# Two transformer blocks on one core: the streamed buffers at other offsets from the weights

## What is computed

```python
# first block
u = rmsnorm(h, norm_mix_pre_w)
q, k, v, z, xbc, dt_raw, gate_logits = split(u @ w_in)
att = dilated_attention(q, k, v) @ w_att_proj      # 12 heads, three dilations
ssm = mamba2_mixer(z, xbc, dt_raw) @ w_ssm_proj    # 32 heads, 8 groups
h = h + rmsnorm((g_att * att + g_ssm * ssm) @ w_out)
f = square(relu(rmsnorm(h) @ w_up)) @ w_down       # 4096 hidden
h = h + rmsnorm(f)
# second block
u_a, u_b, hq, hk, hv, hg = split(rmsnorm(x) @ w_in_2)
y = concat(conformer_conv(u_a, u_b), retention(hq, hk, hv, hg)) @ w_out_2
x = x + rmsnorm(y)
f = (silu(h @ w_ffn_gate_2) * (h @ w_ffn_up_2)) @ w_ffn_down_2   # 2816 hidden
x = x + rmsnorm(f)
x = x + rmsnorm(sigmoid(x @ w_ple_gate_2) * (p @ w_ple_proj_2))
```

## Time and profile before

| | before |
|---|---|
| median of 3 runs | 1813.76 us (1812.43 to 1813.91) |
| the profiled execution's own time | 1813.86 us |
| its span, first to last instruction | 1811.8 us |
| mean granted TensorE clock | 0.998 |
| TensorE busy | 1779.5 us |
| VectorE, ScalarE, GpSimd busy | 841.8, 758.4, 766.4 us |

### The profile page before, as it was taken

How to read it: one execution, slowest core, us unless ns; L and a number is a source line. 1 busy time by engine, 2 the same in 40 slices (tenths; PEclk the granted TensorE clock), 3 DMA queues, 4 the chain that set the end, 5 groups by cost and what they waited for, 6 DMA issues and landing times.

```text
span 1811.8 us, 25066 instructions
## 1 busy us (share of the span) xinstructions
PE 1779.5 (98%) x9062; PEld 1467.6 (81%) x9062; DVE 841.8 (46%) x1577; ACT 758.4 (42%) x1248; POOL 766.4 (42%) x590
## 2 busy tenths in 40 slices
PE   7999999999999999999999999999999999999998
PEld 5777788888888888888888888887778888888877
DVE  4555545677766311273111123899947433320044
ACT  5544554566664322353323233534455332222253
POOL 4322344333333554445444444353233444445543
PEclk9999999999999999999999999999999999999999
DMA  5212233332323222233232322232122232233321
GB/s 186 70 60 83 81 105 111 106 108 95 101 98 128 93 93 97 90 112 111 93 103 93 100 97 82 70 105 70 59 70 73 91 100 97 93 104 105 105 82 47
DMA packets 47803, 170.68 MB, mean 94 GB/s; under 512 B 5312, under 2 KB 7488, under 8 KB 47456
## 3 DMA queue, kind: packets, MB, share of 16 engines
q1 hardware_dynamic: 44352, 156.25, 25.9%
q10 hardware_dynamic: 3360, 13.17, 2.1%
HBM read 167.24 MB, written 2.16 MB: 93 GB/s over the span
## 4 chain that ended last, share of the span: by engine, by line
PE 94%; DVE 4%; ACT 1%; issue 0%; DMA 0%; DVEq 0%; SPq 0%; POOLq 0%; POOL 0%; ACTq 0%
PE bank L395 28%; PE bank L397 28%; PE bank L396 28%; PE bank L574 1%; PE bank L722 1%; PE bank L583 1%; PE bank L596 1%; DVE xs L1879 1%; PE bank L507 1%; PE bank L726 1%; PE bank L706 1%; DVE u_lo L1884 1%; PE bank L822 0%; PE bank L840 0%; PE bank L433 0%
## 5 line engine op out<-in xcount | busy, mean ns | idle before, releaser
L368 POOL TENSOR_TENSOR w_lo<-raw,w_hi 128x512 fp32r<-128x512 f32 x578 | 759.5, 1336 | 1019.2 <-ACT w_hi L1001 1019.0
L395 PE MATMUL bank<-u_hi,w_hi 128*128 128x512 f32 (+1 forms) x1624 | 624.9, 385 | 7.4 <-DVE u_lo L1884 6.5
L397 PE MATMUL bank<-u_hi,w_lo 128*128 128x512 f32 (+1 forms) x1624 | 612.4, 377 | 0.0
L396 PE MATMUL bank<-u_lo,w_hi 128*128 128x512 f32 (+1 forms) x1624 | 611.6, 377 | 0.0
L1001 ACT ACTIVATE w_hi<-raw 128x1024 fp32r<-128x1024 f32 x289 | 303.8, 1052 | 282.5 <-PE bank L397 282.2
L395 PEld LDWEIGHTS bank<-u_hi,w_hi 128*128 128x128 f32 x1624 | 305.5, 188 | 67.9 <-DVE u_lo L1884 7.7
L397 PEld LDWEIGHTS bank<-u_hi,w_lo 128*128 128x128 f32 x1624 | 305.4, 188 | 57.3
L396 PEld LDWEIGHTS bank<-u_lo,w_hi 128*128 128x128 f32 x1624 | 305.8, 188 | 53.5 <-issue 0.5
L395 PE MATMUL bank<-v_hi,w_hi 128*128 128x512 f32 (+1 forms) x368 | 134.4, 365 | 0.2 <-DVE v_lo L2445 0.2
L396 PE MATMUL bank<-v_lo,w_hi 128*128 128x512 f32 (+1 forms) x368 | 133.4, 362 | 0.0
L397 PE MATMUL bank<-v_hi,w_lo 128*128 128x512 f32 (+1 forms) x368 | 133.3, 362 | 0.0
(11 more groups left out here) (320 smaller groups left out, 2175.3 us busy)
## 6 DMA issues: line engine op xcount, KB each, us to landing
raw<-weights SPq DMA_DIRECT2D x289, 512.0 KB, 3.3
bc<-acs ACTq DMA_DIRECT2D x16, 512.0 KB, 4.0
xs<-x SPq DMA_DIRECT2D x4, 512.0 KB, 5.4
xs<-x ACTq DMA_DIRECT2D x1, 2048.0 KB, 7.8
rt<-ret_tables ACTq DMA_DIRECT2D x1, 1536.0 KB, 6.4
out<-xs SPq DMA_DIRECT2D x12, 128.0 KB, 1.8
dist<-att_tables SPq DMA_DIRECT2D x1, 512.0 KB, 10.7
p_raw<-p ACTq DMA_DIRECT2D x1, 512.0 KB, 7.2
```

Of the source, the lines that this page charges most:

```text
L368: return nc.gpsimd.tensor_tensor(w_lo[:, slot, w], raw[:, slot, w], w_hi[:, slot, w].bitcast(F32), ALU.subtract)
L395: mm(dst, w_hi[:, slot, w], hi, start=first, stop=False)
L396: mm(dst, w_hi[:, slot, w], lo, start=False, stop=False)
L397: return mm(dst, w_lo[:, slot, w], hi, start=False, stop=last)
```

## The change

Three areas of `work` are shifted by less than 512 bytes, and with them the tiles in them. No other line changes; the instructions, their order, their semaphores and the DMAs are the same.

- m_at, g_at (and tail, which is g_at + 32 KB) get 256 bytes more: att_acc, mix_hi, logits, p_t, post, hd, acs_h, zz, y_hi, xd, xw, k_t, q_t, b_tok, v_tok, states, v_t, gm and the first half of mix_lo.
- v_at and t_at get 128 bytes more: v_hi, v_lo, wide, glu, tmp, p_raw, the rot and r_ tiles placed from t_at, x_scale, ple_tanh.
- h_hi gets 64 bytes more, h_lo and h_tmp 192.
- raw, w_hi, w_lo, u_hi, u_lo, xs, s_hi, s_lo, the constants, y, y_lo, att_hi, att_lo, dist, bias, cat31, cv, rt, ffn_acc and pj stay.

```diff
-    m_at = work + 32 * K
+    m_at = work + 32 * K + 256
     att_acc = place("att_acc", [P, C8, T], at=m_at)
     mix_hi = place("mix_hi", [P, C8, T], F32R, at=m_at)
...
-    g_at = work + 48 * K
+    g_at = m_at + 16 * K
     post = place("post", [P, 8, T], at=g_at)
...
-    v_at = work + 40 * K
+    v_at = work + 40 * K + 128
     v_hi = place("v_hi", [P, C8, T], F32R, at=v_at)
     v_lo = place("v_lo", [P, C8, T], F32R, at=v_at + 16 * K)
-    t_at = work + 72 * K
+    t_at = v_at + 32 * K
...
-    h_hi = place("h_hi", [P, H2, T], F32R, at=work)
-    h_lo = place("h_lo", [P, H2, T], F32R, at=work + 44 * K)
-    h_tmp = place("h_tmp", [P, T], at=work + 88 * K)
+    h_hi = place("h_hi", [P, H2, T], F32R, at=work + 64)
+    h_lo = place("h_lo", [P, H2, T], F32R, at=work + 44 * K + 192)
+    h_tmp = place("h_tmp", [P, T], at=work + 88 * K + 192)
```

## The result

| | before | after |
|---|---|---|
| median | 1813.76 us (1811.8 to 1814.01, 7 runs) | 1819.26 us (1818.86 to 1820.85, 7 runs) |
| ratio, 95% interval | | 1.0038 [1.0028, 1.0047] |
| span of the profiled execution | 1811.8 us | 1816.9 us |
| mean granted TensorE clock | 0.998 | 0.998 |

The change costs 5.5 us between the medians, 5.1 to 8.5 us by the interval of the ratio. The runs of either kernel lie in two groups some 2 us apart (before 1811.8 and 1812.4 against 1813.5 to 1814.0, after 1818.9 to 1819.3 against 1820.7 to 1820.9), and like against like the change costs 6.8 to 7.0 us. The forecast was no change; the time lies 2.3 us above its range.

The account below looks back on a forecast made before the run. The prediction took TensorE's matmul count times spacing as the bound; 2108 x 0 for moved streams plus 0 for other engines left the time unchanged at 1813.8 us, range 1810.5 to 1817.0.

Parts of the forecast that it names:

- What bounds the kernel: Whole kernel: TensorE busy 1779.5 of 1811.8 us, so time is the number of matmuls times their spacing, 226.7 ns.
- The price of one moved stream: Split products whose stream moves: extra time per matmul, taken as zero, between 13.3 ns gained and 4.4 ns lost.
- 2108 x 0: TensorE's term of the sum: 2108 matmuls with moved streams, each changing by zero.
- The first reason: For zero price: the excess is the same for 512 and 256 columns, so it belongs to the weight load.
- the 32 cycles: Time each split product on TensorE costs beyond its columns, 13.3 ns, for 512 and 256 columns alike.
- The second: For zero price: stream and load addresses drift through some 512 bytes within one load, whatever their distance at the start.
- The third reason: For zero price: weight tiles at 0, 512, 1024 and 1536 modulo 2048 leave h_hi's durations at 389 to 390 ns.
- The bound: Most to lose on moved streams: 4.4 ns each, from products right after the small head products; 9.3 us in all.
- the other engines' part: Other engines' reads and writes of moved buffers: zero price for an offset, bounded at 1.6 us each way.
- C: Rival: streams off a 512-byte boundary touch five blocks instead of four, 9.3 us slower, 1823.1 us; chance 0.05.
- A: Rival: all offsets end collisions of stream and weights, excess vanishes but for 2 ns, 1790.0 us; chance 0.04.
- B: Rival: only one distance ends collisions, 256 giving 1807.5 us or v alone at 128 giving 1799.1; chance 0.04.

Follow-up runs that it names:

- experiment 4: Separate test kernel, no other engine working: 24 matmuls per case at finer distances, column counts, weight widths, turns and bfloat16; 512 columns at distance 244 took 240.4 ns.
- s4x: Section of a separate test kernel with no other engine working: 24 matmuls of 512 columns, stream 4 bytes from the weights modulo 256; spacing 237.0 ns.

## Why the prediction was wrong

**What bounds the kernel** was read rightly: PE at 1.00, 226.7 ns a matmul, and an edit of addresses acts only through that spacing. Its counts of moved matmuls (816, 528 and 288 of 256 columns) are those on which the measured prices multiply out to 6.8 us.

**The price of one moved stream** is the step that failed, the term 2108 x 0 of the sum. "I take zero, for three reasons": measured are 6.6 ns for v at 128, 3.8 for h at 64 and 192, and none for y_hi at 256. The first reason, that the 32 cycles are a property of the load and the same for any number of columns, is not borne out: at distance 0, 504 columns have 42 cycles over, narrower weights raise the excess, weights that stay in place raise it too, and a stream that stays in place lowers it. The second failed outright: drift through 512 bytes within a load was to make the start irrelevant, yet the distance at the start, modulo 256, decides. Why the drift doesn't average is argued only: a mean over a sweep would hold if both reads ran on at a fixed pace, and v's gaps of 229 and 238 ns in turn don't look like one. (The 112 ns of a load was read from products of 128 columns at two cycles, whose columns alone take 107 ns; that it came out right, by 64-column products at 112 ns in experiment 4's kernel, was luck.) The third reason held, distances in whole 512 bytes do nothing, but it said only where the period ends, and 0 was the one value below it that the trace contained; the period is 256. Reading "every distance in the trace costs the same" as "no distance matters" was the mistake: every sample had been taken at the same point.

**The bound was too low as well.** 4.4 ns came from a stretch that had nothing to do with the distance; v costs 6.6, s4x 10 and a distance of 244 14 ns. The total of 9.3 us held against 6.8 by luck, because 476 of the 2108 matmuls lay at 256 and paid nothing and v's 288 of 256 columns got faster. With no row for a resource, the nearest row was no bound. The range of 1810.5 to 1817.0 didn't use even this one: it took the price as nothing and was built from the spread of the runs and the other engines' part.

**The rivals.** C, slower by up to 9.3 us from 1.7 ns a matmul and given 0.05, had the direction and the order of size, and not the mechanism: with 256 bytes a stream touches five blocks of 512 just as with 128, and pays nothing. Nor did it help that all offsets are multiples of 16 bytes: 64, 128 and 192 cost. A and B are refuted by the stretches: 0.691 and 0.700 us a triple in h and v, never 0.646. Their thought, that the 32 cycles at distance 0 depend on addresses, is not refuted: with 256 columns they fell to 16 at distances 112 and 192, and with a stream on one address to 12. Of the other engines' part all holds: VectorE's medians on h_lo and v_lo are 693 and 683 ns, from 693 and 681.

What the row showed of the load beside the stream was 13.3 ns over the columns; the changed kernel's rows show that this depends on the distance between the two reads. The Trainium skill, TensorE: Matmul & The Clock Gate, "Step-by-step: what each phase is for", says that loading the next weights takes no read bandwidth from the running matmul: for float32r the runs disagree, as far as a spacing can tell, with 233 ns against 226.7 by the weights' place alone. The N/2.4 + 2.5 ns of the Trainium skill, TensorE: Matmul & The Clock Gate, "Back-to-back issue gap", agrees with the bfloat16 sections at 215.7 ns and disagrees with float32r at every distance.

**What stays open:** by what mechanism the two reads meet, why the period is 256, why 4 bytes matter, and what picks one of several steady spacings. The distance in bytes between stream and weights, modulo 256, is shown to be the cause of the slowdown; that the two reads meet in the memory is argued. That the dependence goes when either stands still fits it; narrower weights, which cost more at distance 0, don't fit a simple count of meetings.

## What to carry to other kernels

Where TensorE is full with float32r streams of 512 columns, place every streamed tile at a multiple of 256 bytes from the weights, those that take turns too: of the other distances tried alone, 240 and 252 cost 0.1 to 0.3% of a matmul and the rest 1 to 6%, and 240 cost 6% in turn with 0. A trace in which a parameter has one value says nothing on what other values cost; if a change moves that parameter, give the slower side a real chance, and measure the term by itself with a short row of equal instructions.

## What the runs showed of the hardware beside that

- float32r with 512 columns, each with its own load of 128: 226.7 ns at distance 0 modulo 256, 227 to 240 elsewhere, never less while both reads move; with 256 columns 120.0 at distance 0, 113 to 122 elsewhere; with 504 columns 227.6 at distance 0.
- A distance of 244 bytes has 240.4 ns and one of 252 (5.62 - 0.39) / 23 = 227.4; four bytes change a matmul by 10 ns and more.
- fp32 (215.7 ns for 256 columns in each of two records) and dense bfloat16 (215.7 for 512) don't depend on the distance where it was tried: fp32 at 0 and 128, bfloat16 at 0, 64, 128 and 192.
- One distance can have more than one steady spacing: 113.3 and 117.8 ns for 256 columns at 192, and 112 and 213 ns within one section of 128 columns at 0.
